# Rounded operands and one ScalarE table in two attentions of a two-block transformer kernel

## The chip, the cores and the metric

The kernel runs on one core of one Trainium2 chip. The metric is the device time of one execution in microseconds. The kernel before the change takes 2642.69 us (median of 3 runs, 2642.52 to 2645.69).

## What is computed

Two transformer blocks follow each other on x of 256 positions by 2048 channels, in float32. Each has an adaptive norm (scale, shift and gate come from a conditioning vector and a 2048 x 12288 matrix), one wide input projection, two mixers side by side, an output projection and a feed-forward of width 8192. Two pieces of it matter here.

The first block's attention, for 8 heads of 128 channels:

```python
z = einsum('bhqd,bhkd->bhqk', q_blk, kh) * scale
mask = key_pos[None, :] < q_pos[:, None]
log_beta = log_sigmoid(z)
log_1m_beta = log_beta - z
l = where(mask, log_1m_beta, 0.0)
suffix = cumsum(l, axis=3, reverse=True) - l
a = where(mask, exp(log_beta + suffix), 0.0)
out = einsum('bhqk,bhkd->bhqd', a, vh)
...
merged = sigmoid(g_a) * y_a + sigmoid(g_b) * y_b
```

The second block's attention, of 8 heads too, is a softmax over three dilated windows, each masked:

```python
s = where(mask, einsum('brhnqd,brhnkd->brhnqk', qb, kk) / sqrt(Dh), -inf)
p = exp(s - max(s))
```

## The kernel before

All weights pass through the core once, as a stream of pieces of 128 x 1024 floats (512 KB) that SyncE loads into a ring of six buffers (`RAW`, `RAWX`). The big products are made from float32 parts: ScalarE rounds a piece to the type float32r (`feed`, L1045, into `WH`), VectorE subtracts that from the piece and rounds the rest (`item`, L1438, into `WL`), and TensorE adds three products, high x high, high x low and low x high, in float32r (`mm`, L609). One piece is one **tick** j: 12 matmuls of 512 columns on TensorE. There are 848 ticks. `WH` and `WL` have three buffers, so ScalarE may round piece j + 3 only when TensorE has done tick j. Between the weight pieces the stream carries pieces of the two conditioning matrices (`w_ada`), which VectorE alone multiplies and adds into `ACC`; they come in dense groups with gaps. GpSimd then sums `ACC` over the partitions.

Everything else is hung on the ticks by hand. Each engine's program is one loop over j, and at the end of a tick `side` calls whatever is due there. A tick p's side work of TensorE stands behind its 12 matmuls; the answering work of ScalarE and VectorE stands in their tick j = p + 1, behind their weight piece for j + 2. `due` (L127) spreads the 8 heads of an attention two ticks apart over stages s: head h does stage s at tick start + 2h + s. The order on every engine is thus fixed; only semaphores decide how long each waits.

The first attention is `stick`, in the programs of TensorE (L736), ScalarE (L1202) and VectorE (around L1716); it starts at tick `STK0` = 87. For one head:

- stage 0: TensorE turns q and k (four transposes through `ident`, L612), ScalarE copies them out of PSUM with a scale (`QKT`, shown as UQ in the trace).
- stage 2: TensorE makes the scores Z (256 and 128 columns, the part above the diagonal block left out). ScalarE takes the absolute value, then Exp, then Ln (`E1`, also UQ). VectorE adds max(Z, 0) and masks the two diagonal blocks (`E2`, shown as TMP).
- stage 4: TensorE adds the mask (`neglt`, twice 128 columns through `ident`) and the running sums (`nge` x E2, 384 columns, and `nones` x E2, 128 columns) onto Z, all in plain float32. This is called the **sum group** below. ScalarE takes Exp (`E3`, shown as SX).
- stage 6: TensorE makes the head's output, ScalarE and VectorE split it into two parts (`BH`, `BL`).

The constants lie in `ST` (part of SX). Exp and Ln are called by plain activations, and the table for each is loaded by ACT_TABLE_LOAD instructions that the build puts in front. While the attention runs, projection blocks 8 to 11, the gate g_a, come out of PSUM, and ScalarE's `evac` (L1099) takes their Sigmoid on the spot, into `SG`. They are needed when block `aup` is evacuated, from tick 132 on.

The second attention is `dilated` (L865, L1277, L1837), start tick `DIL0` = 541. At its stage 2 TensorE makes the scores and adds the mask `CCN[:, 384:768]` through `ident`, 384 columns in plain float32 (L888). ScalarE issues the loads of `CCN` two ticks ahead (L1373).

Of the kernel before, what the change touches and what calls it, by code (L numbers as in the profile page):

```python
# [14 lines left out]
D = 2048  # L15
S = 256
# [339 lines left out]
def program(nc, I, C, out):  # L356
# [3 lines left out]
    with ExitStack() as ctx:  # L360
# [42 lines left out]

        def ff_memory(tag, stack):
# [33 lines left out]
        CCN = sb("CCN", [128, 768], F32, phase)  # L438
        phase.close()
# [7 lines left out]
        lt, neglt, nge, nones = [ST[:, 128 * i:128 * i + 128] for i in range(4)]  # L447
# [65 lines left out]
        def vc(name, t=0):  # L513
# [20 lines left out]
            "turned", "qk", "z", "softplus", "masked", "e", "a", "o")]  # L534
        s_mg, s_mT, s_mh, s_ml = sem("merged"), sem("m_turned"), sem("m_hi"), sem("m_lo")
# [14 lines left out]
        s_asq, s_att, s_aT, s_ath, s_atl = [sem("attn_" + x) for x in ("squares", "scaled", "turned", "hi", "lo")]  # L550
        s_oag, s_rpn2 = sem("oa_gated"), sem("rope_products")
# [54 lines left out]
        def _(e):  # L606
# [129 lines left out]
            def stick(h, s):  # L736
                qk, e2, e3 = QKT[:, h % 2, :], E2[:, h % 2, :], E3[:, h % 2, :]
# [12 lines left out]
                elif s == 2:  # L750
                    e.wait_ge(s_stq, 2 * h + 2)
                    if h > 1:
                        e.wait_ge(s_st3, h - 1)
                    mm(Z[:, 0:256], kt[:, 0:128], qt, True, False)
                    mm(Z[:, 256:384], kt[:, 128:256], qt[:, 128:256], False, True).then_inc(s_stZ, 1)
                elif s == 4:

                    if h == 0:
                        e.wait_ge(s_stat, 16)
                    e.wait_ge(s_ste, 2 * h + 2)  # L760
                    mm(Z[:, 0:128], ident, neglt, False, False)
                    mm(Z[:, 256:384], ident, neglt, False, False)
                    mm(Z[:, 0:384], nge, e2, False, False)
                    mm(Z[:, 128:256], nones, e2[:, 256:384], False, True).then_inc(s_stE, 1)
                elif s == 6:
                    e.wait_ge(s_st3, h + 1)
                    if h == 0:
                        eng, count = evac_of[bl.at["in1", 7]][1]
                        e.wait_ge(s_ev[eng], count)
                    else:  # L770
                        e.wait_ge(s_bl, 8 + h)
                    mm(O[:, 0:256], UQ[:, 3, 0, h * 128:(h + 1) * 128], e3[:, 0:256], True, False)
                    mm(O[:, 128:256], UQ[:, 3, 1, h * 128:(h + 1) * 128], e3[:, 256:384], False, True).then_inc(s_stO, 1)
# [91 lines left out]
            def dilated(h, s):  # L865
# [14 lines left out]
                elif s == 2:  # L880
                    e.wait_ge(s_dq, h + 1)
                    if h > 0:
                        e.wait_ge(s_dx, 2 * h)
                    else:
                        e.wait_ge(s_cc, 32)
                    mm(Z[:, 0:128], qk[:, 0:128], qk[:, 256:384], True, False)
                    mm(Z[:, 128:384], qk[:, 128:256], qk[:, 256:512], False, False)
                    mm(Z[:, 0:384], ident, CCN[:, 384:768], False, True).then_inc(s_dZ, 1)  # L888
# [52 lines left out]
            def side(p):  # L941
# [3 lines left out]
                for h, s in due(p, STK0, 8, 2, (0, 2, 4, 6)):  # L945
                    stick(h, s)
# [91 lines left out]
        def _(e):  # L1038
# [46 lines left out]
            def evac(q, t):  # L1085
# [3 lines left out]
                if name in ("in1", "part"):  # L1089
# [99 lines left out]

            def pool_copy(g):  # L1190
# [11 lines left out]
            def stick(h, s):  # L1202
                b = h % 2
                qk, e1, e3 = QKT[:, b, :], E1[:, b, :], E3[:, b, :]
                if s == 0:
                    e.wait_ge(s_stT, h + 1)
                    if h == 0:
                        e.wait_ge(s_vc, 4)
                    if h > 1:
# [3 lines left out]
                elif s == 2:  # L1213
                    e.wait_ge(s_stZ, h + 1)
                    if h > 1:
                        e.wait_ge(s_ste, 2 * h - 2)
# [5 lines left out]
                elif s == 4:  # L1222
                    e.wait_ge(s_stE, h + 1)
                    if h > 1:
                        e.wait_ge(s_stO, h - 1)
                    af(e3, PS[:, 5 + b, 0:384], ACT.Exp).then_inc(s_st3, 1)
                elif s == 6:
# [108 lines left out]
            def side(j):  # L1336
# [9 lines left out]
                for h, s in due(p, STK0, 8, 2, (0, 2, 4, 6)):  # L1346
# [26 lines left out]
                if j == HG0 + 64:  # L1373
# [3 lines left out]
                    e.dma_start(CCN[:, 384:768], C["cn"]).then_inc(s_cc, 16)  # L1377
                if j == ANG0 + 6:
# [41 lines left out]
        def _(e):  # L1420
# [295 lines left out]
            def stick(h, s):  # L1716
                b = h % 2
                e1, e2 = E1[:, b, :], E2[:, b, :]
                if s == 2:
# [4 lines left out]
                    if h > 1:  # L1724
                        e.wait_ge(s_stE, h - 1)
# [4 lines left out]
                elif s == 6:  # L1730
# [154 lines left out]
            def side(j):  # L1885
# [12 lines left out]
                for h, s in due(p, STK0, 8, 2, (2, 6)):  # L1898
# [218 lines left out]
```

## Time and profile before

| | |
|---|---|
| median of 3 runs | 2642.69 us |
| the profiled execution: its own time | 2648.83 us |
| its span, first to last instruction | 2646.7 us |
| TensorE busy | 2530.5 us (96%) |
| VectorE busy | 2026.1 us (77%) |
| ScalarE busy | 1296.1 us (49%) |
| mean granted TensorE clock | 0.990 of 2.4 GHz |
| bytes moved | 663.63 MB, mean 251 GB/s |

Busy time of TensorE counts a matmul from its start to its modelled end, and neighbours overlap, so durations of single matmuls do not add up to time. What a matmul costs in a stream is read as the distance from its start to the next one's start. A row of TensorE's time order that merges several instructions gives the first one's start, so the distance to the next row's start is the cost of the whole group. A plain float32 matmul leaves two records. "Idle before" is the time from the last modelled end on that engine to the start, and behind the arrow stands what released it.

### The profile page before, as it was taken

To read this page: it belongs to the slowest core of one execution; us is meant where nothing else is said; L and a number is where in the kernel's file an instruction comes from. 1 tells how busy PE (TensorE), PEld (TensorE's weight loads), DVE (VectorE), ACT (ScalarE), POOL (GpSimd) and SP (SyncE) were. 2 spreads that over 40 slices of the span, in tenths; PEclk is the share of its full clock that TensorE was granted. 3 is DMA by queue.
4 is the path that set the end of the run, shared out by engine and by line. 5 is a ranking of instruction groups with operands and counts; after the bars stand their busy time and mean duration, and the time that the engine had idled before them with its cause. 6 is when DMAs were issued, how large, how long until landed. Compare 5 with 4: busy or idle time off the path is not lost.

```text
span 2646.7 us, 32293 instructions
## 1 busy us (share of the span) xinstructions
PE 2530.5 (96%) x12265; PEld 2106.9 (80%) x12265; DVE 2026.1 (77%) x2308; ACT 1296.1 (49%) x1664; POOL 260.6 (10%) x321
## 2 busy tenths in 40 slices
PE   5999899999899999999998999999999999999998
PEld 4777777777788888888877788887788888888887
DVE  6778868898887888798898788875765566665566
ACT  4544485434454454445535554455455544544453
POOL 1000120202020110202020000450000000020000
PEclk9999999999999999999999999999999999999999
DMA  8898858998898979897967766454567777666654
GB/s 308 311 327 319 273 183 295 332 320 285 278 330 282 348 269 341 264 361 256 340 219 249 253 191 196 142 164 143 183 188 229 227 231 225 228 221 191 190 187 151
DMA packets 298362, 663.63 MB, mean 251 GB/s; under 512 B 20752, under 2 KB 21104, under 8 KB 297184
## 3 DMA queue, kind: packets, MB, share of 16 engines
q1 hardware_dynamic: 294976, 650.21, 72.8%
q0 software_dynamic: 2656, 9.66, 1.0%
q8 instruction: 97, 1.59, 0.2%
q10 hardware_dynamic: 576, 1.70, 0.2%
q14 instruction: 57, 0.47, 0.1%
HBM read 659.39 MB, written 2.10 MB: 250 GB/s over the span
## 4 chain that ended last, share of the span: by engine, by line
PE 77%; DVE 9%; DMA 5%; ACT 4%; issue 4%; SPq 0%; DVEq 0%; POOL 0%; ACTq 0%
PE PS L609 77%; DVE WL L1423 3%; DVE ACC L1431 2%; DMA RAW<-in_w_in 2%; ACT WH L1041 2%; DVE UQ L1423 1%; DMA RAW<-in_w_o 1%; DMA RAWX<-in_w_a_up 1%; DMA RAWX<-in_w_ada 1%; PE PS L612 0%; ACT L1041 0%; DMA RAWX<-in_w_in 0%; DVE acc L1423 0%; ACT UQ L1041 0%; ACT AH L1041 0%
## 5 line engine op out<-in xcount | busy, mean ns | idle before, releaser
L1041 ACT ACTIVATE WH<-RAW 128x1024 fp32r<-128x1024 f32 x567 | 600.1, 1059 | 803.9 <-PE PS L609 614.0
L1423 DVE TENSOR_TENSOR WL<-RAW,WH 128x1024 fp32r<-128x1024 f32 x567 | 705.2, 1245 | 361.7 <-ACT WH L1041 359.8
L609 PE MATMUL PS<-WH,AH 128*128 128x512 f32 x2052 | 817.9, 399 | 31.9 <-DVE WL L1423 17.3
L609 PE MATMUL PS<-WL,AH 128*128 128x512 f32 x2052 | 803.7, 392 | 0.0
L609 PE MATMUL PS<-WH,AL 128*128 128x512 f32 x2052 | 803.6, 392 | 0.0
L609 PE MATMUL PS<-HL,WH 128*128 128x512 f32 x2048 | 728.0, 400 | 8.4 <-issue 4.5
L609 PE MATMUL PS<-HL,WL 128*128 128x256 f32 x2048 | 576.7, 282 | 0.0
L609 PEld LDWEIGHTS PS<-WH,AH 128*128 128x128 f32 x2052 | 388.4, 189 | 126.3 <-DVE WL L1423 33.3
L609 PEld LDWEIGHTS PS<-HL,WH 128*128 128x128 f32 x2048 | 386.7, 189 | 106.4 <-issue 11.9
L609 PEld LDWEIGHTS PS<-WH,AL 128*128 128x128 f32 x2052 | 388.0, 189 | 83.0
L609 PEld LDWEIGHTS PS<-WL,AH 128*128 128x128 f32 x2052 | 388.6, 189 | 78.1 <-issue 1.0
L609 PEld LDWEIGHTS PS<-HL,WL 128*128 128x128 f32 x2048 | 388.9, 190 | 0.5
L1431 DVE SCALAR_TENSOR_TENSOR ACC<-RAW,CS,ACC 128x1024 f32<-128x1024 f32 x265 | 338.5, 1278 | 2.7 <-DMA RAW<-in_w_ada 1.9
L2021 POOL PARTITION_ALL_REDUCE ACC<-ACC x72 | 159.1, 2293 | 1326.7 <-DVE ACC L1431 1326.7
L1041 ACT ACTIVATE WH<-RAWX 128x1024 fp32r<-128x1024 f32 x150 | 158.8, 1058 | 195.5 <-PE PS L609 115.9
L1423 DVE TENSOR_TENSOR WL<-RAWX,WH 128x1024 fp32r<-128x1024 f32 x150 | 187.8, 1253 | 53.3 <-ACT WH L1041 52.4
L1423 DVE TENSOR_TENSOR WL<-RAWY,WH 128x1024 fp32r<-128x1024 f32 x96 | 117.5, 1224 | 71.0 <-ACT WH L1041 70.8
L1041 ACT ACTIVATE WH<-RAWY 128x1024 fp32r<-128x1024 f32 x96 | 101.6, 1059 | 133.5 <-PE PS L609 130.8
L1431 DVE SCALAR_TENSOR_TENSOR ACC<-RAWX,CS,ACC 128x1024 f32<-128x1024 f32 x95 | 121.4, 1278 | 5.7 <-DMA RAWX<-in_w_ada 5.5
L609 PE MATMUL PS<-WX,AH 128*128 128x512 f32 x248 | 77.3, 393 | 1.5 <-DVE AL L1431 1.5
L1423 DVE TENSOR_TENSOR rl<-PS,rl 128x512 f32<-128x512 f32 x64 | 44.0, 688 | 28.2 <-ACT rl L1041 28.2
L1423 DVE TENSOR_TENSOR acc<-PS,acc 128x512 f32<-128x512 f32 x96 | 65.6, 683 | 0.0
(241 smaller groups left out, 1959.2 us busy)
## 6 DMA issues: line engine op xcount, KB each, us to landing
RAW<-in_w_ff SPq DMA_DIRECT2D x335, 512.0 KB, 4.3
RAW<-in_w_ada SPq DMA_DIRECT2D x284, 512.0 KB, 5.0
RAW<-in_w_in SPq DMA_DIRECT2D x192, 512.0 KB, 4.6
RAWX<-in_w_ada SPq DMA_DIRECT2D x100, 512.0 KB, 5.3
RAWY<-in_w_ff SPq DMA_DIRECT2D x96, 512.0 KB, 4.1
RAWX<-in_w_ff SPq DMA_DIRECT2D x81, 512.0 KB, 5.2
RAWX<-in_w_in SPq DMA_DIRECT2D x48, 512.0 KB, 5.2
RAW<-in_w_out SPq DMA_DIRECT2D x32, 512.0 KB, 3.6
```

The lines of the kernel that those rows point to most:

```text
L609: return e.matmul(o, l, r, start=start, stop=stop, skip_group_check=True)
L1041: return e.activation(o, i, f, **kw)
L1423: return e.tensor_tensor(o, a, b, op)
L1431: return e.scalar_tensor_tensor(out=o, in0=a, scalar=s, in1=b, op0=op0, op1=op1)
L2021: e.partition_all_reduce(part, part, 128, bass.bass_isa.ReduceOp.add).then_inc(s_red, 1)
```

## The change

It has four parts. (1) Both attentions get rounded (float32r) copies of the constants: `STR` and `IR` for the first, made by ScalarE at the first head, `CNR` and `IR2` for the second, made by ScalarE at tick 541. The mask products use them. (2) In the first attention VectorE splits `E2` into two float32r parts, `E2H` and `E2L`, in a new stage 3, and the sum group multiplies both, six matmuls instead of four. The stages behind it move by one: the sum group to 5, the output to 7. (3) ScalarE loads the table set `natural_log_exp_and_others` once ahead of the first head. (4) The four Sigmoid pairs of g_a move out of `evac` into `first_gate`, at ticks 111 to 114, behind the last head. The core of the diff:

```diff
             def stick(h, s):   # TensorE
...
-                elif s == 4:
+                elif s == 5:
 
                     if h == 0:
-                        e.wait_ge(s_stat, 16)
-                    e.wait_ge(s_ste, 2 * h + 2)
-                    mm(Z[:, 0:128], ident, neglt, False, False)
-                    mm(Z[:, 256:384], ident, neglt, False, False)
-                    mm(Z[:, 0:384], nge, e2, False, False)
-                    mm(Z[:, 128:256], nones, e2[:, 256:384], False, True).then_inc(s_stE, 1)
-                elif s == 6:
+                        e.wait_ge(s_str, 1)
+                    e.wait_ge(s_sth, h + 1)
+                    high, low = E2H[:, h % 2, :], E2L[:, h % 2, :]
+                    neglt_r, nge_r, nones_r = [STR[:, 128 * i:128 * i + 128] for i in range(3)]
+                    mm(Z[:, 0:128], IR[:, :], neglt_r, False, False)
+                    mm(Z[:, 256:384], IR[:, :], neglt_r, False, False)
+                    mm(Z[:, 0:384], nge_r, high, False, False)
+                    mm(Z[:, 128:256], nones_r, high[:, 256:384], False, False)
+                    e.wait_ge(s_stl, h + 1)
+                    mm(Z[:, 0:384], nge_r, low, False, False)
+                    mm(Z[:, 128:256], nones_r, low[:, 256:384], False, True).then_inc(s_stE, 1)
+                elif s == 7:
...
             def dilated(h, s):   # TensorE
...
                     else:
-                        e.wait_ge(s_cc, 32)
+                        e.wait_ge(s_ccr, 1)
...
-                    mm(Z[:, 0:384], ident, CCN[:, 384:768], False, True).then_inc(s_dZ, 1)
+                    mm(Z[:, 0:384], IR2[:, :], CNR[:, :], False, True).then_inc(s_dZ, 1)
...
             def evac(q, t):   # ScalarE
...
-                    elif name == "in1" and 8 <= n < 12:
-                        e.wait_ge(s_ev["dve"], evac_of[q][t][1])
-                        af(dst, dst, ACT.Sigmoid).then_inc(s_sga, 1)
...
+            def first_gate(n):
+
+                for t in range(2):
+                    eng, count = evac_of[bl.at["in1", n]][t]
+                    e.wait_ge(s_ev[eng], count)
+                    af(in1_home(n, t), in1_home(n, t), ACT.Sigmoid).then_inc(s_sga, 1)
...
             def stick(h, s):   # ScalarE
...
                 if s == 0:
+                    if h == 0:
+
+                        e.preload_act_table_set("natural_log_exp_and_others")
                     e.wait_ge(s_stT, h + 1)
                     if h == 0:
                         e.wait_ge(s_vc, 4)
+
+                        e.wait_ge(s_stat, 16)
+                        af(STR[:, :], ST[:, 128:512], ACT.Copy)
+                        af(IR[:, :], ident, ACT.Copy).then_inc(s_str, 1)
...
                 if j in (WO + 24, IN2 - 4, OB + 12):
                     preload_sqrt()
+                if 0 <= j - STK0 - 24 < 4:
+                    first_gate(8 + j - STK0 - 24)
...
+                if j == DIL0:
+                    e.wait_ge(s_cc, 32)
+                    af(CNR[:, :], CCN[:, 384:768], ACT.Copy)
+                    af(IR2[:, :], ident, ACT.Copy).then_inc(s_ccr, 1)
...
             def stick(h, s):   # VectorE
...
-                elif s == 6:
+                elif s == 3:
+
+                    e.wait_ge(s_ste, 2 * h + 2)
+                    if h > 1:
+                        e.wait_ge(s_stO, h - 1)
+                    e.tensor_copy(E2H[:, b, :], e2).then_inc(s_sth, 1)
+                    e.wait_ge(s_sth, h + 1)
+                    tt(E2L[:, b, :], e2, f32(E2H[:, b, :]), ALU.subtract).then_inc(s_stl, 1)
+                elif s == 7:
```

How the order of instructions moves. First **TensorE, the sum group of head 0** (TMP is E2, SX holds the constants, SQ is `ident`). Before, with the next two heads' scores and transposes right behind it:

```order
L609 MATMUL PS<-WH,AL 128x512
L609 MATMUL PS<-SX,SQ 128x128 x2
L609 MATMUL PS<-TMP,SX 128x384
L609 MATMUL PS<-TMP,SX 128x128
L609 MATMUL PS<-UQ 128x256
L609 MATMUL PS<-UQ 128x128
L612 MATMUL PS<-SQ,UQ 128x128 x4
L609 MATMUL PS<-WH,AH 128x512
```

After the change, in a tick of its own, one tick later:

```order
L622 MATMUL PS<-STR,IR 128x128 x2
L622 MATMUL PS<-E2H,STR 128x384
L622 MATMUL PS<-E2H,STR 128x128
L622 MATMUL PS<-E2L,STR 128x384
L622 MATMUL PS<-E2L,STR 128x128
```

The four plain matmuls have become six rounded ones, and the scores and transposes of the next heads no longer stand directly behind them.

Second **ScalarE, one head's round** (UQ is QKT and E1, SX is E3). Before, head 1's Abs, Exp and Ln behind head 0's last Exp:

```order
L1041 ACT_TABLE_LOAD
L1041 ACTIVATE SX<-PS 128x384
L1041 ACTIVATE UQ<-PS 128x384
L1041 ACTIVATE UQ<-UQ 128x384
L1041 ACT_TABLE_LOAD
L1041 ACTIVATE UQ<-UQ 128x384
L1041 ACTIVATE UQ<-PS,SM 128x256
L1041 ACTIVATE UQ<-PS,VC 128x256
```

After the change, the like piece:

```order
L1059 ACTIVATE SX<-PS 128x384
L1059 ACTIVATE WH<-RAW 128x1024
L1059 ACTIVATE UQ<-PS 128x384
L1059 ACTIVATE UQ<-UQ 128x384 x2
L1059 ACTIVATE UQ<-PS,SM 128x256
L1059 ACTIVATE UQ<-PS,VC 128x256
```

No table load is left between the heads, and the last Exp of a head stands one weight piece ahead of the next one's Abs. ScalarE's whole program has 19 table loads, 40 before.

Third **VectorE, the split of E2** after the change:

```order
L1464 SCALAR_TENSOR_TENSOR TMP<-PS,UQ 128x384
L1456 TENSOR_TENSOR TMP<-TMP,SX 128x2x128
L1456 TENSOR_TENSOR WL<-RAW,WH 128x1024
L1456 TENSOR_TENSOR SG<-PS,SG 128x512
L1456 TENSOR_TENSOR BL<-PS,BH 128x256
L1769 CAST E2H<-TMP 128x384
L1456 TENSOR_TENSOR E2L<-TMP,E2H 128x384
```

The cast and the subtraction are new; they stand one weight piece behind the mask, and behind the split of an earlier head's output.

## Rows read from the trace of the kernel before

**Rows 1.** Page, part 1 (busy us) and part 5 (groups: busy, mean ns), whole program.
```profile
PE 2530.5 (96%) x12265; PEld 2106.9 (80%) x12265; DVE 2026.1 (77%) x2308; ACT 1296.1 (49%) x1664; POOL 260.6 (10%) x321
...
L1041 ACT ACTIVATE WH<-RAW 128x1024 fp32r<-128x1024 f32 x567 | 600.1, 1059 | 803.9 <-PE PS L609 614.0
L1423 DVE TENSOR_TENSOR WL<-RAW,WH 128x1024 fp32r<-128x1024 f32 x567 | 705.2, 1245 | 361.7 <-ACT WH L1041 359.8
...
L1431 DVE SCALAR_TENSOR_TENSOR ACC<-RAW,CS,ACC 128x1024 f32<-128x1024 f32 x265 | 338.5, 1278 | 2.7 <-DMA RAW<-in_w_ada 1.9
```
**Rows 2.** Stretches: length, then busy of PE, PEld, DVE, ACT, POOL, clock, DMA share, GB/s.
```profile
331.00:345.00 14.00, 12.69 (x60) 10.37 (x60) 11.61 (x13) 8.87 (x13) 0.00 (x0) 1.00 0.97 343
363.00:381.00 18.00, 16.23 (x82) 13.55 (x83) 8.59 (x13) 17.06 (x26) 2.02 (x2) 1.00 0.39 118
...
460.00:480.00 20.00, 18.54 (x79) 14.26 (x78) 18.53 (x18) 9.09 (x10) 0.00 (x0) 1.00 1.01 376
```
**Rows 3.** Waits from 331 to 417 us: total, times, longest.
```profile
DVE TMP L1431 <- ACT UQ L1041: 23.5, 8, 4.2
PE PS L609 <- DVE TMP L1423: 5.2, 5, 1.3
ACT WH L1041 <- DMA RAW<-in_w_in: 4.1, 2, 2.4
```
**Rows 4.** ScalarE, costliest groups from 325 to 450 us.
```profile
L1041 ACT ACT_TABLE_LOAD x23 | 29.5, 1283 | 0.4
L1041 ACT ACTIVATE UQ<-UQ 128x384 f32<-128x384 f32 x16 | 8.4, 525 | 0.3
```
**Rows 5.** TensorE in order of time, the stalls: start, length, instruction, [idle].
```profile
343.54 0.39 PE L609 MATMUL PS<-WH,AL 128*128 128x512 f32 x1
345.23 0.68 PE L609 MATMUL PS<-SX,SQ 128*128 128x128 f32 x4 [1.30 <-DVE TMP L1423]
...
363.42 0.71 PE L609 MATMUL PS<-SX,SQ 128*128 128x128 f32 x4 [0.88 <-DVE TMP L1423]
...
373.56 0.71 PE L609 MATMUL PS<-SX,SQ 128*128 128x128 f32 x4 [1.35 <-DVE TMP L1423]
...
391.34 0.71 PE L609 MATMUL PS<-SX,SQ 128*128 128x128 f32 x4 [0.46 <-DVE TMP L1423]
...
401.33 0.71 PE L609 MATMUL PS<-SX,SQ 128*128 128x128 f32 x4 [1.18 <-DVE TMP L1423]
```
**Rows 6.** TensorE in order of time, the sum group of a head without a stall.
```profile
382.20 0.61 PE L609 MATMUL PS<-SX,SQ 128*128 128x128 f32 x4
...
383.51 0.82 PE L609 MATMUL PS<-UQ 128*128 128x256 f32 x4
```
**Rows 7.** TensorE in order of time, rounded matmuls of several widths near 1722 us.
```profile
1722.07 0.48 PE L609 MATMUL PS<-CT,LFH 128*128 128x512 f32 x1
1722.39 0.39 PE L609 MATMUL PS<-CT,LFL 128*128 128x512 f32 x1
1722.62 0.34 PE L609 MATMUL PS<-CT,LFH 128*128 128x384 f32 x1
...
1722.97 0.22 PE L609 MATMUL PS<-CT,LFH 128*128 128x128 f32 x1
1723.03 0.27 PE L609 MATMUL PS<-CT,LFL 128*128 128x128 f32 x1
1723.14 0.29 PE L612 MATMUL PS<-SQ,HG 128*128 128x128 f32 x1
```
**Rows 8.** TensorE in order of time, the mask product of the second attention.
```profile
1746.37 0.81 PE L609 MATMUL PS<-CCN,SQ 128*128 128x384 f32 x2
1747.02 0.60 PE L612 MATMUL PS<-SQ,QK 128*128 128x128 f32 x4
```
**Rows 9.** VectorE product of 384 columns; time to landing of the mask's load.
```profile
L1423 DVE TENSOR_TENSOR KP<-KP,CCN x8: 547/551/552, 1756.6 to 1815.2; 128x384 f32<-128x384 f32 x8
DMA to landing us min/median/max: 3.9/4.0/4.0
```

More of the change, by code:

```diff
@@ L402, in program @@
         phase.close()
+        phase = ExitStack()
+        sb("to_E1", [128, 2 * KT * S + 1024], F32, phase)
+        E2L = sb("E2L", [128, 2, 384], F32R, phase)
+        sb("to_E3", [128, 7 * 1024 - 768 + 2 * D + 2 * 512 + 512], F32, phase)
+        E2H = sb("E2H", [128, 2, 384], F32R, phase)
+        STR = sb("STR", [128, 384], F32R, phase)
+        IR = sb("IR", [128, 128], F32R, phase)
+        phase.close()
         def ff_memory(tag, stack):
@@ L438, in program @@
         CCN = sb("CCN", [128, 768], F32, phase)
+        CNR = sb("CNR", [128, 384], F32R, phase)
+        IR2 = sb("IR2", [128, 128], F32R, phase)
         phase.close()
@@ L446, in program @@
         E3 = SX[:, 512:1280].rearrange("p (b x) -> p b x", b=2)
-        lt, neglt, nge, nones = [ST[:, 128 * i:128 * i + 128] for i in range(4)]
+        lt = ST[:, 0:128]
         xT = XT0[:, :].rearrange("p (k s) -> p k s", s=S)
@@ L534, in program @@
             "turned", "qk", "z", "softplus", "masked", "e", "a", "o")]
+        s_str, s_sth, s_stl = sem("stick_constants"), sem("stick_hi"), sem("stick_lo")
         s_mg, s_mT, s_mh, s_ml = sem("merged"), sem("m_turned"), sem("m_hi"), sem("m_lo")
@@ L550, in program @@
         s_asq, s_att, s_aT, s_ath, s_atl = [sem("attn_" + x) for x in ("squares", "scaled", "turned", "hi", "lo")]
+        s_ccr = sem("cc_rounded")
         s_oag, s_rpn2 = sem("oa_gated"), sem("rope_products")
@@ L736, in stick @@
             def stick(h, s):
-                qk, e2, e3 = QKT[:, h % 2, :], E2[:, h % 2, :], E3[:, h % 2, :]
+                qk, e3 = QKT[:, h % 2, :], E3[:, h % 2, :]
                 T, Z, O = PS[:, 4, :], PS[:, 5 + h % 2, :], PS[:, 7, :]
@@ L944, in side @@
                     (pool_map if (p - POOL0) % 2 else pool_mix)((p - POOL0) // 2)
-                for h, s in due(p, STK0, 8, 2, (0, 2, 4, 6)):
+                for h, s in due(p, STK0, 8, 2, (0, 2, 5, 7)):
                     stick(h, s)
@@ L1215, in stick @@
                     if h > 1:
-                        e.wait_ge(s_ste, 2 * h - 2)
+                        e.wait_ge(s_stE, h - 1)
                     af(e1, PS[:, 5 + b, 0:384], ACT.Abs).then_inc(s_stx, 1)
@@ L1221, in stick @@
                     af(e1, e1, ACT.Ln, bias=1.0).then_inc(s_stx, 1)
-                elif s == 4:
+                elif s == 5:
                     e.wait_ge(s_stE, h + 1)
-                    if h > 1:
-                        e.wait_ge(s_stO, h - 1)
                     af(e3, PS[:, 5 + b, 0:384], ACT.Exp).then_inc(s_st3, 1)
-                elif s == 6:
+                elif s == 7:
                     e.wait_ge(s_stO, h + 1)
@@ L1345, in side @@
                     e.dma_start(G[:, :], I["b_ada"][0:1, 2 * D:3 * D].partition_broadcast(128)).then_inc(s_gb0, 16)
-                for h, s in due(p, STK0, 8, 2, (0, 2, 4, 6)):
+                for h, s in due(p, STK0, 8, 2, (0, 2, 5, 7)):
                     stick(h, s)
@@ L1724, in stick @@
                     if h > 1:
-                        e.wait_ge(s_stE, h - 1)
+                        e.wait_ge(s_sth, h - 1)
+                        e.wait_ge(s_stl, h - 1)
                     stt(e2, PS[:, 5 + b, 0:384], 0.0, e1, ALU.max, ALU.add).then_inc(s_ste, 1)
@@ L1729, in stick @@
                     tt(d, d, lt.unsqueeze(1).broadcast_to([128, 2, 128]), ALU.mult).then_inc(s_ste, 1)
-                elif s == 6:
+                elif s == 3:
[5 more added lines that the diff above has]
+                    tt(E2L[:, b, :], e2, f32(E2H[:, b, :]), ALU.subtract).then_inc(s_stl, 1)
+                elif s == 7:
                     e.wait_ge(s_bh, 8 + h + 1)
@@ L1897, in side @@
                     qk_norm((j - QKN0) // 2, (j - QKN0) % 2)
-                for h, s in due(p, STK0, 8, 2, (2, 6)):
+                for h, s in due(p, STK0, 8, 2, (2, 3, 7)):
                     stick(h, s)
```

## The prediction

> **What bounds the kernel now.** I read the page first. TensorE is busy 96% of the span, VectorE 77%, ScalarE 49% [rows 1]. So a change pays only where it takes time off TensorE itself, or takes away one of its waits. Table loads on ScalarE alone are worth nothing.
>
> Then the table of stretches over the first attention. Ahead of it the queues are full: DMA share 0.97 and 343 GB/s in 331 to 345 us. In the attention the load drops to 118 GB/s while ScalarE works 17.06 of 18 us [rows 2], and TensorE's granted clock is 1.00 in all three rows, its level of 2.4 GHz. Here ScalarE, not the stream of weights, holds the others up. The list of waits says how: VectorE waits 23.5 us in 8 pieces, one per head, for ScalarE's Exp and Ln (UQ), and TensorE waits 5.2 us in 5 pieces for VectorE's masked result (TMP) [rows 3]. The cause stands in the groups of ScalarE: 23 table loads of 1283 ns, 29.5 us in all, against 8.4 us for the 16 activations that they serve most [rows 4].
>
> Last, TensorE in order of time. The first stalled head shows what a stall costs in the stream: the last matmul of the tick starts at 343.54, and the next could start 0.23 later, at 343.77, but starts at 345.23 [rows 5]. That is 1.46 us, a little more than the 1.30 idle that the row names, since the idle is counted from the modelled end. The other four rows name 0.88, 1.35, 0.46 and 1.18. With 0.16 more for each, the five stalls cost 5.17 + 0.8 = 6.0 us.
>
> **The change part by part.**
>
> *Stalls.* The order rows leave one table load ahead of head 0 and one for the Sigmoids behind head 7, so 21 of 23 go: 21 x 1.283 = 27 us off ScalarE. Besides, the sum group is asked for one tick later. What TensorE needs is now: scores at the end of tick p+2; Abs, Exp, Ln (0.5 us each [rows 4]), VectorE's addition and mask (0.9 together by [rows 9]) in its next tick; cast and subtraction one tick on; the sum group only at the end of tick p+5. I walk the slowest path, from the end of tick p+3: ScalarE's weight rounding 1.06, VectorE's rest 1.25, two `w_ada` pieces at 1.28 [rows 1], the split of an output (0.4 estimated from the 0.55 of [rows 9] at 256 instead of 384 columns), cast and subtraction 0.8 (below), in sum 6.1 us. TensorE has ahead of it the output of 384 plain columns (0.65 as in [rows 8]) and another head's sum group (0.8), two ticks of 12 x 0.227 = 2.73, the scores (0.65 too) and four transposes (0.4), some 7.9 us. Some 1.8 us are to spare, so all five stalls go: **-6.0**, bounds -6.4 (the first matmul behind a stall starts 0.1 slower) and -3.0 (half of them reappear).
>
> *Sum group.* Before, it takes 383.51 - 382.20 = 1.31 us per head [rows 6], 1.7 ns for each of its 768 columns, about four times the 0.227 / 512 = 0.44 ns of a rounded one. Rounded matmuls of these widths stand in the trace at 1722 us: two of 384 columns take 1722.97 - 1722.62 = 0.35, two of 128 columns 0.06 and 0.11, and the first after a plain one costs 0.32 instead of 0.23, so 0.09 extra [rows 7]. The new group is 4 x (0.06 to 0.11) + 2 x 0.175 + 0.09 = 0.68 to 0.88 us. I take 0.78, the middle, as only one of the narrow matmuls has each price. It saves 0.53 per head, times 8: **-4.2**, bounds -3.4 and -5.0. The extra 0.09 of the tick's next weight matmul falls away, but now an even and an odd tick each have one change of type, so this cancels.
>
> Here a page speaks for the dear end. The Trainium skill, "TensorE: Matmul & The Clock Gate", section on LDWEIGHTS, says that loading weights takes about the number of columns over 1.2 GHz, 107 ns for 128, whatever follows. Estimated by that page, a 128-column matmul with weights of its own can't be under 0.107, and the sum group saves 3.6 us instead of 4.2. The trace has one start-to-start of 0.06 beside one of 0.11, and does not decide it.
>
> *VectorE's two new operations.* The cast of 384 columns isn't in the trace; the subtraction is bounded above by the 0.55 us of a product of 384 columns that also reads two tiles and writes one [rows 9], the cast by 0 and the same 0.55. I take 0.35 (between) and 0.55, less 0.1 by which neighbours on VectorE overlap, 0.8 us per head. Their cover is VectorE's own wait of 23.5 us. Per head (two ticks, some 7.9 us after the change) VectorE needs two weight rests 2.5, addition and mask 0.9, the split 0.4, up to two `w_ada` pieces 2.6 and the new 0.8, in sum 7.2. Cost: 0, bounds 0 and +2. With the cover gone they would cost 6.4.
>
> *ScalarE's copies.* `STR` (384 columns, 0.5) and `IR` (0.3) with the table load 1.28 come ahead of head 0's copies, where ScalarE waits for the stream (4.1 us in 2 pieces, [rows 3]). `CNR` and `IR2` at tick 541 wait for a load that lands in 4.0 us [rows 9] and was issued two ticks, over 5.4 us, before. Cost 0, bounds 0 and +0.5.
>
> *Second attention.* The mask product takes 1747.02 - 1746.37 = 0.65 us [rows 8]. Rounded, 0.175 + 0.09 = 0.27 [rows 7]. It stands in a stretch where TensorE is busy without a gap, so all of it counts: 8 x 0.38 = **-3.1**, bounds -2.5 and -3.8 (no extra for the change of type).
>
> *The Sigmoids.* Eight, of 512 columns each, go to ticks 111 to 114, read first at tick 132: 20 ticks are cover enough. 0.
>
> *What is given back.* Around the attention the stream of weights is itself near its limit: 343 GB/s before, 376 after [rows 2]. Ticks that TensorE finishes sooner there must wait for data: ScalarE waits up to 2.4 us for pieces at the beginning [rows 3]. The first stall and the last stall lie at those edges. I give back 1.0 of their 2.8 us, bounds 0 and 2.8: **+1.0**.
>
> Sum: -6.0 - 4.2 - 3.1 + 1.0 = **-12.3 us**. The profiled execution took 2648.8 us with a span of 2646.7; I expect some 2636 for a like one. The median of the runs is 6.1 us lower, 2642.7, and the difference carries over: 2642.7 - 12.3 = **2630.4**.
>
> **The rivals.**
>
> *A. The stream takes it back.* TensorE gets to the dense groups of `w_ada` sooner and finds no data there. For it: the DMA share of 0.97 and 1.01 on the two sides. Against: between the heads the load was 118 GB/s [rows 2], and the ring is full again within one head. Its price is 1.46 + 1.34 of stalls and the work of two heads, 1.0: 2642.7 - 13.3 + 3.8 = 2633.2.
>
> *B. Narrow rounded matmuls pay full price.* If 128 rounded columns cost what plain ones do, 4 x 128 x 0.44 = 0.23, the sum group is 4 x 0.23 + 0.35 + 0.09 = 1.36 us and 0.05 longer than before, 0.4 for 8 heads: 2642.7 - 6.0 + 0.4 - 3.1 + 1.0 = 2635.0. [rows 7] speaks against it.
>
> *C. VectorE ends last, slower.* The cast stands in order behind BL, which waits for TensorE's output product of an earlier head and for ScalarE's copy of it. If VectorE is so late with its weight rests that the cast comes only when TensorE already stands at the sum group, each head stalls by ScalarE's copy (0.5) with its hand-over, VectorE's split (0.4) and the new 0.8, and once more by the weight rest that it then is late with (up to 1.25): 1.7 to 2.95, 2.3 in the mean. 8 x 2.3 = 18.4 us against 7.3 of saved work: 2642.7 + 11.1 = 2653.8. It decides once VectorE is over 1.8 us behind the walk above. Against it: VectorE is busy only 8.59 of 18 us in the middle of the attention [rows 2].
>
> *D. The change does not do what it says*: the build could put loads back between Exp and Ln. The order rows exclude it, 19 loads are left. That leaves execution time of Exp or Ln under the joint table; 0.1 us more each would be hidden.
>
> **How the numbers follow.** A measurement of this kernel tells about 0.2% from no change, 5.3 us. My forecast has 0.72, A 0.12, B 0.05, all faster by more. A mixture of A, B and new stalls that ends within 5.3 us, 0.08; C and the like 0.03. So faster 0.89, same 0.08, slower 0.03. The range: below, -6.4 - 5.0 - 3.8 without anything given back is -15.2, 2627.5, and 1 us for the spread of medians; above, it takes in A, B and half of the stalls back, -3.0 - 3.4 - 2.5 + 2.8 = -6.1. That is 2626.5 to 2636.6. All cases of the range have one sign.
>
> **What would show it.** Right: in the profile after, no wait of TensorE for VectorE's TMP or E2 tiles; ScalarE's table loads down to 19; from sum group to sum group 7.9 us; the sum group 0.7 to 0.9 long; the mask product of the second attention 0.2 to 0.3; the stretch of the first attention some 9 to 10 us shorter. Wrong: TensorE waiting for E2L or E2H (C), more waits for weight rests in the ticks around the attention (A), or starts of 0.2 us between 128-column products with STR (B).

## The result, and the profile after

The changed kernel takes 2630.31 us (median of 4 runs, 2628.31 to 2631.06), the kernel before 2642.64 us beside it (4 runs too). The ratio is 0.9942, with a 95% interval of 0.9928 to 0.9956; measured again with more runs (below) it is 0.9946, 0.9931 to 0.9960. Both mean 14 to 15 us less, with some 4 us of uncertainty; the difference of the first two medians, 12.3 us, lies inside.

The page after, parts 1 and 5:

```profile
PE 2520.9 (96%) x12241; PEld 2103.1 (80%) x12241; DVE 2031.0 (77%) x2324; ACT 1270.8 (48%) x1647; POOL 265.3 (10%) x321
```

Against [rows 1], TensorE is busy 9.6 us less, ScalarE 25.3 less and VectorE 4.9 more. The table of stretches over like parts of the first attention (columns as in [rows 2]):

```profile
327.00:341.00 14.00, 13.68 (x69) 11.65 (x70) 13.97 (x16) 9.45 (x15) 0.00 (x0) 1.00 0.97 345
359.00:377.00 18.00, 18.00 (x96) 15.24 (x95) 12.22 (x20) 9.86 (x18) 0.23 (x1) 1.00 0.47 142
445.00:465.00 20.00, 19.14 (x83) 15.09 (x82) 18.23 (x17) 8.91 (x10) 0.00 (x0) 1.00 1.00 354
```

The middle row is the one to compare with 363 to 381 us of [rows 2]: TensorE is busy for all 18 us instead of 16.23, with 96 instead of 82 matmul records, and ScalarE needs 9.86 us instead of 17.06. The waits from 327 to 406 us, and the groups of ScalarE in and around the attention:

```profile
ACT UQ L1059 <- PE PS L622: 15.7, 6, 2.8
ACT WH L1059 <- PE PS L622: 11.4, 11, 2.4
...
PE PS L625 <- DVE UQ L1456: 1.6, 1, 1.6
```
```profile
L1059 ACT ACTIVATE UQ<-UQ 128x384 f32<-128x384 f32 x16 | 8.4, 526 | 0.5
L1230 ACT ACT_TABLE_LOAD x1 | 1.3, 1283 | 0.0
L1059 ACT ACT_TABLE_LOAD x1 | 1.3, 1283 | 0.0
```

The direction of waiting has turned. In [rows 3] VectorE waited 23.5 us for ScalarE and TensorE 5.2 us for VectorE; now ScalarE waits 27 us for TensorE, and TensorE's one wait of 1.6 us is the one ahead of head 0, which was there before. Exp and Ln take 526 ns under the joint table, 525 before [rows 4], and the load is 1283 ns. TensorE in order of time, one head:

```profile
350.84 0.39 PE L622 MATMUL PS<-WH,AL 128*128 128x512 f32 x1
351.07 0.81 PE L622 MATMUL PS<-SX,UQ 128*128 128x256 f32 x4
351.64 0.42 PE L622 MATMUL PS<-STR,IR 128*128 128x128 f32 x2
351.89 0.45 PE L622 MATMUL PS<-E2H,STR 128*128 128x384 f32 x2
352.18 0.45 PE L622 MATMUL PS<-E2L,STR 128*128 128x384 f32 x2
352.47 0.44 PE L622 MATMUL PS<-WH,AH 128*128 128x512 f32 x1
...
355.04 0.39 PE L622 MATMUL PS<-WH,AL 128*128 128x512 f32 x1
355.32 0.89 PE L622 MATMUL PS<-UQ 128*128 128x256 f32 x4
356.05 0.60 PE L625 MATMUL PS<-SQ,UQ 128*128 128x128 f32 x4
```

The sum group takes 352.47 - 351.64 = 0.83 us; it was 1.31 [rows 6]. The output product ahead of it takes 0.57 us instead of 0.65. The scores in the next tick take 0.73 us here, where 0.65 was usual, and the matmul ahead of them 0.28 instead of 0.23; so it is in four of the eight heads. In the second attention the mask product is:

```profile
1728.66 0.82 PE L622 MATMUL PS<-QP 128*128 128x128 f32 x4
1729.13 0.53 PE L622 MATMUL PS<-CNR,IR 128*128 128x384 f32 x1
1729.49 0.60 PE L625 MATMUL PS<-SQ,QK 128*128 128x128 f32 x4
```

It takes 0.36 us instead of 0.65 [rows 8], and the scores ahead of it 0.47 instead of 0.65: 0.47 us less per head.

**Where the profiled executions differ otherwise.** The spans are 17.4 us apart, more than the change. 3.9 us of it is there before the first changed instruction: head 0's transposes start at 331.24 before and at 327.32 after. Over all fourteen traces of this study that start lies between 324.8 and 331.2 us. On the other side, the stretch of the first output projection behind the second attention has two lengths, 57 us in seven of the fourteen traces and 60 to 61.5 in the other seven, in kernels with and without the change. In all seven long ones the granted clock falls to 1.2 GHz for a part of this stretch, in none of the seven short ones. The profile after is a long one; a row of the stretch table shows the clock there:

```profile
1800.00:1810.00 10.00, 7.28 (x22) 5.46 (x21) 2.01 (x3) 1.78 (x3) 0.00 (x0) 0.69 0.31 110
```

TensorE had waited 0.9 and 1.1 us and then ran at 1.2 GHz for a part of the time from 1800 to 1804 us, and once more behind a wait of 2.7 us that ended at 1806.90. The same three waits (0.9, 1.1 and 2.8 us) stand in the profile before, without a fall. So I compare stages, each by its own start and end, not spans.

### The profile page after: what moved, and what is told of

Read it like the earlier page. It is cut to its first block, busy times and chain, and to the rows that moved or that the text cites. A ratio compares the mean times of both kernels' runs of the same rounds, so it can differ in the third digit from the quotient of the medians.

```text
span 2629.3 us, 32244 instructions
## 1 busy us (share of the span) xinstructions
PE 2520.9 (96%) x12241; PEld 2103.1 (80%) x12241; DVE 2031.0 (77%) x2324; ACT 1270.8 (48%) x1647; POOL 265.3 (10%) x321
## 4 chain that ended last, share of the span: by engine, by line
PE 79%; DVE 9%; DMA 5%; ACT 3%; issue 3%; SPq 0%; DVEq 0%; POOL 0%; ACTq 0%
PE PS L622 78%; DVE WL L1456 3%; DVE ACC L1464 2%; ACT WH L1059 2%; DMA RAW<-in_w_in 2%; DVE UQ L1456 1%; DMA RAW<-in_w_o 1%; DMA RAWX<-in_w_a_up 1%; PE PS L625 1%; DMA RAWX<-in_w_ada 1%; DMA RAWX<-in_w_o 0%; DVE acc L1456 0%; ACT AH L1059 0%; ACT L1059 0%; ACT XT L1059 0%
## 5 line engine op out<-in xcount | busy, mean ns | idle before, releaser
L622 PE MATMUL PS<-WH,AH 128*128 128x512 f32 x2052 | 816.0, 398 | 30.5 <-DVE WL L1456 16.2
```

The costliest lines, as they stand in the source:

```text
L622: return e.matmul(o, l, r, start=start, stop=stop, skip_group_check=True)
```

## The experiments

Twelve runs follow, of the change itself and of ten more kernels. In three groups of them the kernel before was timed beside them, with medians of 2645.7, 2645.7 and 2646.7 us. That is 3 to 4 us more than the 2642.6 from which the first four expectations count, so I go by the ratio to before, and those expected times are to be read as distances from 2642.6.

The first attention's length is read from the trace in every one: from head 0's transposes to the last output product, less 2.7 us for the one tick more where the stages are 5 and 7. **It is 85.7 us before and 78.6 - 2.7 = 75.9 after.**

**Second attention's mask alone.** Before, with

```diff
-                    mm(Z[:, 0:384], ident, CCN[:, 384:768], False, True).then_inc(s_dZ, 1)
+                    mm(Z[:, 0:384], IR2[:, :], CNR[:, :], False, True).then_inc(s_dZ, 1)
```

and the two copies for it.

> Before, with only the second attention's mask product rounded. My theory: 3.1 us off as forecast, up to 3.8, since the profile after shows 0.47 us less from scores to transposes for each of 8 heads; so 2638.8 to 2639.5 against 2642.6. Rival: the gain is given back behind the attention, because TensorE still waits 2.7 us for the first split of the mixer's output and, as in the profile after, goes on at a granted clock of 0.69 for 10 us (3.0 us lost); then 2641.8 to 2642.6.

Ratio to before 0.9984 (0.9975 to 0.9993), 2642.3 against 2645.7 us: 4.2 us less by the ratio, 1.9 to 6.6 by its interval. From the first mask product to the mixer's projection it takes 60.5 us instead of 63.9. Its projection stretch was a short one, 57.2 us. The rival falls: the gain is not given back. Nor does the rounded mask bring the long stretch about: of the nine traces with it four are long, of the five with the plain mask three.

**Tables alone.** Before, with

```diff
+                        e.preload_act_table_set("natural_log_exp_and_others")
...
-                    elif name == "in1" and 8 <= n < 12:
-                        e.wait_ge(s_ev["dve"], evac_of[q][t][1])
-                        af(dst, dst, ACT.Sigmoid).then_inc(s_sga, 1)
...
+                if 0 <= j - STK0 - 24 < 4:
+                    first_gate(8 + j - STK0 - 24)
```

> Before, with only the table set loaded ahead and the gate's Sigmoids moved; the sum group stays plain and in stage 4. Theory: the table loads alone make the stalls, so all five go (6.0 us), and the stream runs ahead in the attention, which the profile after shows as 3.2 us between ticks 108 and 128: 2633.4 to 2636.6. Rival: it is the extra tick before the sum group that removes the stalls; then over half of the waits of TensorE for TMP stay and the time is 2639 or more.

Ratio 0.9962 (0.9949 to 0.9975), 2637.95 us: 10 us less, 7 to 13 by the interval. The attention takes 79.1 us, 6.6 less than before, and TensorE waits for TMP nowhere. So the extra tick is not what removes the stalls. But this edit takes out two things at once, the loads and the Sigmoids with their waits for VectorE, and in the kernel before four of the five stalls stand in just those rounds that hold a Sigmoid. ScalarE ahead of the stall at 373.56:

```profile
364.00 1.28 ACT L1041 ACT_TABLE_LOAD   x1
366.03 0.63 ACT L1041 ACTIVATE SG<-SG 128x512 f32<-128x512 f32 x1 [0.74 <-DVE SG L1423]
366.57 1.04 ACT L1041 ACTIVATE WH<-RAW 128x1024 fp32r<-128x1024 f32 x1
```

The load for the Sigmoid, the wait for VectorE and the Sigmoid take 2.6 us of this round (364.00 to 366.57), as much as the two loads for Exp and Ln that every round has. Of the four heads whose rounds hold no Sigmoid only head 0 stalls. That speaks for the Sigmoids as the larger part. But no run has the Sigmoids moved and the loads between Exp and Ln left, or the other way round, so how much each of the two is worth is not shown.

**No tables.** The changed kernel, with the loads and the Sigmoids put back:

```diff
-                        e.preload_act_table_set("natural_log_exp_and_others")
...
+                    elif name == "in1" and 8 <= n < 12:
+                        e.wait_ge(s_ev["dve"], evac_of[q][t][1])
+                        af(dst, dst, ACT.Sigmoid).then_inc(s_sga, 1)
```

> The changed kernel with the table loads back (43 of them) and the Sigmoids back where the gate comes out of PSUM; rounding, split and later stages stay. Theory: with three loads a head ScalarE needs about 2 x 0.96 + 0.8 + 1.4 + 0.8 + 3.85 = 8.8 us per head against TensorE's 7.9 and sets the pace, so only the second attention's 3.1 to 3.8 and little of the first's is left: 2636 to 2640. Rival: the extra tick covers the loads; then TensorE's saved work and the stalls are gained without the tables: 2629 to 2632.

Ratio 1.0016 (1.0007 to 1.0024), 2650.7 us: slower than before, although the second attention's gain is in it. Both expectations miss. The attention takes 101.0 us: TensorE stalls at the scores of six heads, 18.7 us in all and 7.4 at the longest. The next kernel has stalls at the same place with the stage numbers alone changed, and shows why.

**Later stages alone.** Before, with the stage numbers changed on all three engines:

```diff
-                for h, s in due(p, STK0, 8, 2, (0, 2, 4, 6)):
+                for h, s in due(p, STK0, 8, 2, (0, 2, 5, 7)):
                     stick(h, s)
```

> Before, with only the sum group and the output moved one tick later (stages 5 and 7), nothing rounded, table loads as the build puts them (43). Theory: ScalarE needs 8.8 us per head against TensorE's 8.5 and stalls it instead: 2641 to 2646. Rival: the extra tick alone removes the five stalls: 2636 to 2637.

Ratio 1.0056 (1.0044 to 1.0068), 2660.1 us, 15 us slower; another miss, on the far side. The attention takes 105.6 - 2.7 = 102.9 us. Two rows of its waits from 331 to 430 us:

```profile
PE PS L609 <- ACT SX L1041: 16.2, 6, 5.9
ACT UQ L1041 <- PE PS L609: 12.0, 5, 4.3
```

TensorE waits for E3, but at which instruction? TensorE and then ScalarE in order of time around the longest:

```profile
365.51 1.62 PE L609 MATMUL PS<-UQ 128*128 128x256 f32 x4 [5.85 <-ACT SX L1041]
366.92 1.06 PE L612 MATMUL PS<-SQ,UQ 128*128 128x128 f32 x4
```
```profile
359.89 1.28 ACT L1041 ACT_TABLE_LOAD   x1
362.66 0.63 ACT L1041 ACTIVATE SG<-SG 128x512 f32<-128x512 f32 x1 [1.48 <-DVE SG L1423]
363.19 0.37 ACT L1041 ACTIVATE BH<-PS 128x256 fp32r<-128x256 f32 x1
363.58 1.28 ACT L1041 ACT_TABLE_LOAD   x1
364.87 0.49 ACT L1041 ACTIVATE SX<-PS 128x384 f32<-128x384 f32 x1
```

It is not the output product but the scores (UQ) of the head two further on. They write the PSUM bank that this Exp reads, and there are two such banks for eight heads. With the later stages the Exp stands one tick ahead of those scores, before it was two. A load for the Sigmoid, its wait for VectorE, and the load back stand in between, and the transposes on which ScalarE's next round rests stand behind the scores: each engine waits for the other in turn. I had summed ScalarE's load over a head (8.8 us) and not followed who waits for whom.

The waits are not all of it. Behind the two longest TensorE runs at 1.2 GHz; the row of the stretch behind the first (columns as in [rows 2], the clock 0.52 of 2.4 GHz):

```profile
363.00:370.00 7.00, 4.49 (x14) 3.92 (x15) 1.65 (x2) 6.05 (x9) 0.00 (x0) 0.52 0.42 124
```

Of the 17 us that the attention grows, 11 are idle time of TensorE (16.2 against 5.2 before); some 5 are matmuls at half speed, estimated from the 10 us or so of matmuls that lie in the two slow stretches.

**Tables and later stages**, the edits of *tables alone* and *later stages alone* together and nothing rounded, to see whether the later stages are dear only with the loads and the Sigmoids in place:

> Before, with the table set loaded ahead, the Sigmoids moved and the later stages 5 and 7, nothing rounded or split. Theory: the 14 us that the later stages cost with the loads in place (TensorE's scores wait for the Exp that frees their PSUM bank, one tick ahead instead of two, and ScalarE for the transposes behind those scores) are only there with the loads; with them gone the later stages cost nothing: like the tables alone, 2636 to 2638. Rival: the later stages cost TensorE part of it anyway: 2641 or more.

Ratio 0.9963 (0.9951 to 0.9975), 2636.7 us, as the tables alone. The attention falls from 102.9 to 83.0 - 2.7 = 80.3 us. In the trace it is still 1.1 us over the tables alone, and the waits name nothing for it: now two ticks per head have a change of type. The scores take 0.73 us in four heads here too (366.29 to 367.02, for example), though nothing is rounded, so this goes with the later stages; why, no run shows.

**No later stage.** The changed kernel with stages 4 and 6 and the split right behind the mask:

```diff
-                elif s == 3:
-
                     e.wait_ge(s_ste, 2 * h + 2)
```

> The changed kernel with the sum group and output back in stages 4 and 6; the split of E2 stands right behind its mask on VectorE, in the same tick. Theory: without table loads the path from the scores to the sum group is short enough for two ticks too (Abs, Exp, Ln 1.4, addition and mask 0.9, split 0.9, a weight piece's rounding and rest on each engine ahead: 5.5 us of some 6.2), so no or one or two short stalls: 2630 to 2632. Rival: the later stage is needed for the split, each head stalls by up to 0.9 us: 2634 to 2638.

Ratio 0.9933 (0.9921 to 0.9946), 2628.7 us; the attention takes 75.1 us, without any stall. So the later stages are not needed once the loads and the Sigmoids are gone. By the trace they cost 0.8 us, less than the runs can tell.

**First attention only**, the change without the second attention's part, beside **the change again**:

```diff
-                    mm(Z[:, 0:384], IR2[:, :], CNR[:, :], False, True).then_inc(s_dZ, 1)
+                    mm(Z[:, 0:384], ident, CCN[:, 384:768], False, True).then_inc(s_dZ, 1)
```

> The changed kernel with the second attention's mask product plain again. Theory: parts add up, so it is slower than the change by 3.1 to 3.8 us: 2633.4 to 2634.1. Rival: the lower clock behind the second attention takes the gain back: within 1 us of the change.

> The changed kernel once more, as the base for the three kernels beside it. 2630.3, as measured.

2634.2 and 2630.5 us, ratios to before 0.9957 (0.9945 to 0.9969) and 0.9946 (0.9931 to 0.9960). 3.7 us between the medians, as expected; the ratios' intervals overlap. The traces give it clearer: 63.9 against 60.5 us in the second attention, 78.6 in the first with both.

**VectorE's cover.** The changed kernel with

```diff
-                    e.tensor_copy(E2H[:, b, :], e2).then_inc(s_sth, 1)
-                    e.wait_ge(s_sth, h + 1)
+                    for i in range(5):
+                        if i > 0:
+                            e.wait_ge(s_sth, 5 * h + i)
+                        e.tensor_copy(E2H[:, b, :], e2).then_inc(s_sth, 1)
+                    e.wait_ge(s_sth, 5 * h + 5)
```

> The changed kernel with VectorE's cast of E2 made five times, one after the other, 4 x 0.46 = 1.8 us more per head on VectorE, 14.7 us in all. Theory: VectorE has 1.8 us to spare on the path to the sum group and little more in its load per head (7.2 of 7.9 us only in dense groups, which cover three of the heads), so a few heads stall: 2631 to 2636. Rival: the cover was thinner than I worked out and VectorE already sets the pace: plus 12 us or more, 2642. Second rival: it is far thicker, since VectorE waits for nothing any more: no change.

2633.3 us beside 2630.5, ratio 0.9954 (0.9942 to 0.9966), which the runs can't tell from the change. In the traces the attention grows from 78.6 to 81.9 us for 15.0 us of added work, and only two heads stall; from the waits of that stretch, and VectorE in order of time at these two heads:

```profile
PE PS L622 <- DVE E2H L1772: 2.1, 2, 1.2
```
```profile
347.41 4.96 DVE L1772 CAST E2H<-TMP 128x384 fp32r<-128x384 f32 x5
358.52 3.27 DVE L1772 CAST E2H<-TMP 128x384 fp32r<-128x384 f32 x5
```

The burden is not the even 1.8 us per head that was meant. I had taken a mean of 0.46 us for the cast, but seven of the eight casts of the profile after take 0.35 us and one takes 1.25. Six heads here get 1.6 us more, and none of them stalls. The two heads above get 3.7 and 2.9 us more, and stall by 1.24 and 0.90. So the cover is 1.6 us or more, and by estimate (added time less stall) 2.5 and 2.0 us in these two heads: what I had worked out, 1.8, or a little more.

**An early first split.** The trace after showed something beside the change. At the start of the recurrent mixer TensorE waits; here in the repeated run of the changed kernel:

```profile
1485.78 0.50 PE L622 MATMUL PS<-CT,LFH 128*128 128x512 f32 x1 [2.32 <-ACT LFH L1059]
1487.04 0.59 PE L622 MATMUL PS<-CT,LFL 128*128 128x512 f32 x1 [0.76 <-DVE LFL L1456]
1487.42 0.63 PE L622 MATMUL PS<-CT,LFH 128*128 128x512 f32 x1
```

The input of that split is ready some ten ticks earlier, but it stands on ScalarE behind a weight piece whose data are late:

```profile
1484.47 1.06 ACT L1059 ACTIVATE WH<-RAW 128x1024 fp32r<-128x1024 f32 x1 [3.97 <-DMA RAW<-in_w_in]
1485.43 0.29 ACT L1059 ACTIVATE LFH<-HK 128x128 fp32r<-128x128 f32 x1
```

The edit, on both engines:

```diff
+                if j == HG0 - 5:
+                    hgrn(0, 0)
                 for i, s in due(p, HG0, 16, 4, (0, 1, 5, 7)):
-                    hgrn(i, s)
+                    if (i, s) != (0, 0):
+                        hgrn(i, s)
```

> The changed kernel, with the first split of the logarithms of the second block's recurrent mixer (LFH and LFL of its first piece) five ticks earlier on ScalarE and VectorE. In both profiles TensorE waits there for ScalarE, which waits for data of a weight piece ahead of it (2.6 and 0.8 us after the change), and then runs a stretch of matmuls at 0.43 us instead of 0.23. Theory: both waits and the slow stretch go, 3.4 + up to 3 us: 2624 to 2627. Rival: the matmuls wait for the stream in the next ticks instead: 2629 to 2630.

> The changed kernel with the early first split once more, to halve the uncertainty of its gain over the change: 2628.3 as measured, 2 to 5 us under the change.

2628.3 and 2626.2 us, ratios to before 0.9936 (0.9924 to 0.9947) and 0.9920 (0.9908 to 0.9933), mean 0.9928 against 0.9944 of the change: about 4 us, with an uncertainty of some 3.5 by the four intervals. The first run gained only 2.2 us on the change beside it, less than the 3.4 to 6.4 that I expected, and lay closer to the rival. Both waits are gone and the clock stays up behind them. The same place, and the granted clock of the place in the change and in the second of these runs:

```profile
1477.83 0.39 PE L622 MATMUL PS<-CT,LFH 128*128 128x512 f32 x1
1478.06 0.39 PE L622 MATMUL PS<-CT,LFL 128*128 128x512 f32 x1
```
```profile
1478.00:1488.00 10.00, 6.65 (x24) 4.84 (x23) 9.01 (x23) 5.07 (x7) 0.00 (x0) 0.83 0.83 259
```
```profile
1476.00:1486.00 10.00, 10.00 (x46) 8.24 (x45) 9.28 (x24) 5.83 (x7) 0.00 (x0) 1.00 0.81 270
```

From the first ticks of this projection (the first use of WX) to the second attention it takes 326.0 us in this run and 325.1 in the other, instead of 330.2 and 329.8 in the change. All eleven traces without the early split lie between 327.6 and 331.4, mean 329.6; the three with it, the next kernel among them, between 324.6 and 326.0. So it is worth 4.4 us by the traces. The waits themselves were 3.1 to 3.4 us, but not all of that is gained: 11 us further on a new wait stands, which the change does not have,

```profile
1488.92 0.49 PE L622 MATMUL PS<-XT 128*128 128x128 f32 x2 [1.58 <-DVE KP L1459]
```

and the next wait behind it is shorter (0.47 us instead of 0.91). TensorE's idle time over the whole stretch falls by 2.0 us. The rest goes with the granted clock: in the change it is 0.83 in the 10 us shown above and again some 50 us later, in this run only the second time, in the other run with the early split neither time. A granted clock of 0.83 over 10 us is 1.7 us lost, by estimate.

**Merged masks.** That, and

```diff
-                    mm(Z[:, 0:128], IR[:, :], neglt_r, False, False)
-                    mm(Z[:, 256:384], IR[:, :], neglt_r, False, False)
+                    blocks = Z[:, 0:384].rearrange("p (a t) -> p a t", t=128)[:, 0:3:2, :]
+                    mm(blocks, IR[:, :], neglt_r.unsqueeze(1).broadcast_to([128, 2, 128]), False, False)
```

> The changed kernel with the early first split, and with the two 128-column mask products of a sum group made one of 256 columns (8 matmuls fewer). Theory: 0.25 us for the pair becomes some 0.15, 0.8 us in all, under what the runs can tell: 2627 to 2629. Rival: none on the other side but noise; a strided output in PSUM could cost more than it saves, then 2629 to 2631.

2623.4 us, ratio 0.9911 (0.9897 to 0.9924), over 3 us less than either side expected. It is 23 us under before, and its interval lies wholly under the change's. Of its margin over the change the traces show the early split (4 to 5 us) and 0.9 us in the attention, 77.7 instead of 78.6. The sum group is 350.50 - 349.78 = 0.72 us, where it was 0.83, and 8 x 0.11 is the 0.9:

```profile
349.78 0.36 PE L622 MATMUL PS<-STR,IR 128*128 128x256 f32 x1
349.98 0.40 PE L622 MATMUL PS<-E2H,STR 128*128 128x384 f32 x2
350.22 0.45 PE L622 MATMUL PS<-E2L,STR 128*128 128x384 f32 x2
350.50 0.45 PE L622 MATMUL PS<-WH,AH 128*128 128x512 f32 x1
```

The merged product takes 0.20 us instead of 0.25 for the pair, and the group of 384 and 128 columns behind it 0.24 instead of 0.29. Of the 3 us by which it beat the early split alone no more than this 0.9 is shown; the intervals of the two overlap.

## Why the prediction was right

It said 2630.4 us for the median, 12.3 us less, by a sum of four terms. Term by term:

*Stalls, -6.0.* Shown, at -6.6: that is what the attention loses when the loads and the Sigmoids go, and the waits for TMP are gone. The five stalls themselves are the 6.0; the other 0.5 is that the first matmuls behind a stall were slower, which I had only as a bound: a sum group behind a stall took 1.42 us, one without a stall 1.31. Two reasons that I gave need mending. I counted the extra tick among them, and that was wrong: it does not help, and with loads and Sigmoids in place it costs 17 us of attention. And I named the loads as the cause and put the moved Sigmoids at 0, whereas four of the five stalls stood in rounds with a Sigmoid; the two parts of the change were only tested together. The walk along the path said that 1.8 us were to spare per head, and the burden on VectorE agrees. The order and the tables belong together: whoever had moved the stages first would have seen that step fail.

*Sum group, -4.2.* Measured 79.1 - 75.9 = -3.2. The group itself came out at 0.83 us for my 0.78, so 0.48 per head is saved, 3.8 in all. The pair of masks takes 0.25, each group of 384 and 128 columns 0.29, for which I had 0.24 to 0.29. It is not the narrow matmuls that are dear. TensorE around one of them:

```profile
352.12 0.22 PE L622 MATMUL PS<-E2H,STR 128*128 128x128 f32 x1
352.18 0.39 PE L622 MATMUL PS<-E2L,STR 128*128 128x384 f32 x1
```

The 128 columns of E2H start 0.06 us before the next matmul, and the 384 ahead of them 0.23 before these (351.89 to 352.12), where I had 0.175. The Trainium skill, "TensorE: Matmul & The Clock Gate", section "LDWEIGHTS (loading the stationary operand)", gives the number of columns over 1.2 GHz for a weight load, 107 ns for 128. Estimated by that page the group is 0.87 and the term -3.5 (the prediction's 3.6 is a slip). The measured 0.83 lies between that and my 0.78, and a distance of 0.06 stands beside it, so 0.107 is not the least distance here.

The remaining 0.6 is the neighbourhood: I let the changes of type cancel, and they don't. Over eight heads the output product is 0.6 us shorter, but the scores in four heads and the matmuls ahead of them cost 0.6 more, the first weight matmul behind the group 0.4 (0.28 instead of 0.23), and 0.2 is spread thinly over the others. Without the later stages the term is 79.1 - 75.1 = -4.0.

*Second attention, -3.1.* Measured -3.8 by the rows of a head (8 x 0.47), -3.4 from the first mask product on and -3.5 from the first scores on, in every trace with the rounded mask. My 0.27 us for the mask was too little, it is 0.36, outside the 0.2 to 0.3 that I had named as a sign; but the plain scores ahead of it now pass in 0.47 instead of 0.65, which I had not looked for.

*VectorE's two operations, 0.* Right. The cast takes 0.35 us (once 1.25) and the subtraction 0.56, as I took them, and nobody waits for them.

*Given back to the stream, +1.0.* Not found, and rival A with it. From the last output product to the first product with `BH`, ticks 108 to 128, it takes 59.5 us before and 58.7 with the second mask alone; in the kernels without stalls it takes 56.3 to 58.4, the missing tick added. If anything the stream is better off: in [rows 2] its share fell to 0.39 while VectorE stood waiting, and it has 0.47 now. That cause is argued, not shown: two kernels without the tables gave 56.9 and 58.0, so most of it may be chance.

So the terms measured are -6.6, -3.2, -3.5 and 0 or less, -13.3 or a little more in sum; the ratios say -14 to -15, and the medians of the first runs -12.3. That the forecast met a median to 0.1 us is luck of about 2 us, and in the sum a term too large (the sum group) stands against two too small and a loss that did not come. The sign, the places and roughly the sizes are not luck. Of the other signs, the attention is 9.8 us shorter and 19 loads are left, as said; from sum group to sum group it takes 8.2 us in the middle of the attention, not 7.9. Of the other rivals, C (VectorE ends last) is refuted by the burden, B (narrow matmuls at the plain price) by the 0.25 us of the pair, and D by the two loads in the attention's rows and the 526 ns.

## What to carry to other kernels

An engine that is half idle over the whole program can still be the one that sets the pace in one stage: read the stretch, not the share, and then follow the one wait of the bounding engine back. When a stage is moved to a later tick, look not only at what it waits for but at what it frees: here a PSUM bank came free one tick late, and a harmless-looking delay cost 17 us until the table loads and Sigmoids in its way were gone. When an edit takes out two things from one engine's round, as here loads and Sigmoids, try them one by one before naming the cause. Read a mean beside its smallest and largest value: one cast of 1.25 us made 0.46 out of 0.35. And a short wait of TensorE can be paid twice, once as the wait and once as the slower matmuls behind it, so the cheap repair of a single ordering fault (a split that stood behind a late weight piece) was worth 4 us.

## What the runs showed of the hardware

The distance between rounded matmuls depends on what surrounds them more than I had assumed: 128 columns cost 0.06 and 0.11 in one place [rows 7] and 0.06 to 0.14 in the sum group; 384 columns 0.23 in the sum group, 0.17 behind the merged mask; 256 columns 0.20. A plain product of 384 columns ahead of a rounded one takes 0.47 or 0.57 against 0.65 ahead of a plain one.

The granted clock fell in one stretch behind waits of 0.9, 1.1 and 2.7 us that left it at 1.00 in other executions, and this makes 3 to 4 us of difference between two runs of one kernel (57.2 and 60.2 us in the change, 57.2 and 61.5 with the early split).

ScalarE's table load leaves no gap: 1283 ns in all 40 loads of the kernel before, and where nothing else is awaited the next activation starts 1.29 us after the load does (363.58 to 364.87 in the rows above).

VectorE's cast of 384 columns takes 0.35 us, but some take up to 1.25: one of eight in the profile after, eight of forty over 0.6 in the burdened kernel. All these slow ones fall into the 16 to 17 us in which GpSimd sums `ACC` over the partitions (344.1 to 361.2 us in the burdened kernel), though not every cast in that time is slow. That GpSimd is the cause is not shown.
